# Second mixer's projections in a two-layer encoder: plain 32-bit matrix products replaced by three products over split operands

## The reference, cut to what matters

```python
def gla_mixer(h, w_in, w_gate2, b_gate2, gla_norm_g, w_out):     # h: (1, 512, 1024), the second mixer
    proj = h @ w_in                                              # (1024, 3088)
    q, k, v, g, z = jnp.split(proj, [512, 1024, 2048, 3072], axis=-1)
    log_a = jax.nn.log_sigmoid(z @ w_gate2 + b_gate2) / 16.0
    ...                      # chunks of 64 rows: state = state * decay + k_dec.T @ v;  o = q @ state
    o = o * lax.rsqrt(jnp.mean(o * o, axis=-1, keepdims=True) + EPS) * gla_norm_g
    o = o.reshape(B, S, 1024) * jax.nn.silu(g)
    return o @ w_out                                             # (1024, 1024)

# the trunk
x = x + even_mixer(rmsnorm(x, ln_mix[0]), ...)   # first mixer
x = x + peer(rmsnorm(x, ln_ffn[0]), ...)         # first expert stage
x = x + gla_mixer(rmsnorm(x, ln_mix[1]), ...)    # second mixer
x = x + peer(rmsnorm(x, ln_ffn[1]), ...)         # second expert stage
return rmsnorm(x, ln_final)
```

## Time and profile before

| | |
|---|---|
| Time, median of 3 runs | 2854.05 us (2853.29 to 2854.83) |
| Span of the profiled execution | 2852.1 us, 1.95 us under that median |
| PE busy | 2831.2 us (99%) |
| DVE busy | 2282.9 us (80%) |
| ACT busy | 1015.6 us (36%) |
| POOL busy | 750.5 us (26%) |

### The profile page before, as it was taken

The page is one execution under the profiler, slowest core; times in us unless marked ns, Lnnn a source line. Parts: engine busy times, 40 slices in busy tenths (PEclk is TensorE's granted clock), DMA queues, the critical chain, the costliest instruction groups (busy, mean ns, idle before and its releaser), DMA issues.

```text
span 2852.1 us, 39729 instructions
## 1 busy us (share of the span) xinstructions
PE 2831.2 (99%) x14626; PEld 1528.0 (54%) x14722; DVE 2282.9 (80%) x4310; ACT 1015.6 (36%) x1350; POOL 750.5 (26%) x518
## 2 busy tenths in 40 slices
PE   9999999999999999999999999999999999999999
PEld 5455555556666444444544465555566664444444
DVE  6955899997888999999611258999978888999996
ACT  2253232334555333333321232223345543333333
POOL 0000233421111554545000002333211115455450
PEclk9999999999999999999999999999999999999999
DMA  4213677867997999999321236777679979999993
GB/s 158 89 47 142 242 280 279 293 239 273 320 311 291 398 395 393 398 400 396 134 89 59 76 142 234 276 291 277 240 285 311 310 286 403 391 398 398 392 397 152
DMA packets 214835, 776.01 MB, mean 272 GB/s; under 512 B 15508, under 2 KB 101912, under 8 KB 194744
## 3 DMA queue, kind: packets, MB, share of 16 engines
q1 hardware_dynamic: 50096, 416.89, 38.2%
q0 software_dynamic: 73728, 268.47, 25.5%
q10 hardware_dynamic: 90888, 89.14, 9.0%
HBM read 681.90 MB, written 92.54 MB: 272 GB/s over the span
## 4 chain that ended last, share of the span: by engine, by line
PE 93%; issue 2%; PEld 1%; DVE 1%; DMA 1%; ACT 1%; DVEq 0%; POOL 0%; PEldq 0%; SPq 0%; ACTq 0%
PE ps L1819 29%; PE ps L1750 12%; PE ps L1749 12%; PE ps L1748 12%; PE ps L1722 8%; PE ps L1411 5%; PE ps L1402 4%; PE ps L1432 4%; PE ps L1801 2%; PE ps L1800 2%; PEld ps L1819 1%; PE ps L1758 1%; DMA arena<-in_ur,arena 1%; PE ps L1528 1%; PE ps L1465 0%
## 5 line engine op out<-in xcount | busy, mean ns | idle before, releaser
L1819 PE MATMUL ps<-arena 128*128 128x512 bf16 x4488 | 985.3, 379 | 6.7 <-DVE arena L1272 1.5
L500 POOL DMA_INDIRECT arena<-in_ur,arena x256 | 351.8, 1374 | 1582.8 <-DVE arena L1110 928.0
L1819 PEld LDWEIGHTS ps<-arena 128*128 128x128 bf16 x4584 | 448.2, 98 | 542.8 <-issue 3.5
L1083 DVE TENSOR_TENSOR arena<-arena 128x1024 bf16<-128x1024 f32 x512 | 611.3, 1220 | 116.6 <-ACT arena L723 93.7
L1750 PE MATMUL ps<-xnh,arena 128*128 128x384 bf16 x2048 | 667.6, 326 | 0.0
L1749 PE MATMUL ps<-xnl,arena 128*128 128x384 bf16 x2048 | 667.5, 326 | 0.0
L1748 PE MATMUL ps<-xnh,arena 128*128 128x384 bf16 x2048 | 667.4, 326 | 0.0
L723 ACT ACTIVATE arena<-arena 128x1024 bf16<-128x1024 f32 x512 | 524.2, 1048 | 120.0 <-PE ps L1819 98.8
L500 POOL DMA_INDIRECT arena<-in_v,arena x256 | 397.7, 1554 | 401.8 <-DVE x_res L1119 341.6
L1119 DVE SCALAR_TENSOR_TENSOR x_res<-arena,x_res 128x1024 f32<-128x1024 f32 x256 | 328.5, 1283 | 21.1 <-issue 0.9
L749 ACT ACTIVATE arena<-ps 128x384 f32<-128x384 f32 x256 | 125.8, 491 | 565.3 <-PE ps L1750 565.3
(11 more groups left out here) (219 smaller groups left out, 2294.0 us busy)
## 6 DMA issues: line engine op xcount, KB each, us to landing
arena<-in_v SPq DMA_DIRECT2D x64, 2048.0 KB, 10.3
arena<-in_u SPq DMA_DIRECT2D x62, 2048.0 KB, 10.2
h_scratch<-arena ACTq DMA_DIRECT2D x60, 768.0 KB
arena<-h_scratch SPq DMA_DIRECT2D x60, 768.0 KB, 8.6
arena<-gate_scratch SPq DMA_DIRECT2D x64, 640.0 KB, 6.8
arena<-in_wmix SPq DMA_DIRECT2D x14, 2048.0 KB, 8.0
gate_scratch<-xnT ACTq DMA_DIRECT2D x10, 2048.0 KB
gate_scratch<-arena ACTq DMA_DIRECT2D x10, 2048.0 KB
```

What stands on the lines that cost most here:

```text
L500: pool.indirect_dma_start(ring[n % NBUF], None, ur_d[L] if g < P else vr_d[L], at).then_inc(gat_in[n % NBUF], 16)
L1083: dve.tensor_tensor(lo[:, s], raw[s // TPG][:, s % TPG], hi[:, s], ALU.subtract).then_inc(lo_ready, 1)
L1819: last = pe.matmul(ps[:, 2 + 2 * tt + dh], c, v[:, TPG * s + q, dh * 512:(dh + 1) * 512], start=start and c is ch and v is hi, stop=stop a ...
```

## The change

The projections of `mixer1` (not z, not the small products, not the scan) are no longer one 32-bit product. Each operand is split into a high part, rounded to the type float32r, and the rest. The product is high x high, high x rest, and rest x high, all in float32r: 24 matmuls for a unit where there were 8 of 32 bits.

- ACT rounds each weight block in four pieces of 128 x 1024 (`weights_hi`), DVE subtracts in four pieces, in place over the block (`weights_lo`). Both stand at fixed places of the two engines' programs.
- The normalized tokens go to `x_hi`, written as float32r by the same instructions as before; DVE then makes the rest from PSUM (`norm_rest`), eight instructions a tile. The heads' outputs are treated in the same way (`heads_out`, four more instructions a tile on DVE, for both halves).
- The z unit stays 32-bit, with the tokens in two parts: 16 matmuls for 8.
- A unit waits for all four high pieces of its block before its first matmul, and for all four rest pieces before its last eight.
- The buffers in the arena are laid out anew. SP's first load of the second expert stage's query weights waits for the readouts (`go_done`), not for `kdec_ready`. It still stands behind the loads of blocks 9 to 15 in SP's program.

```diff
+        w_lo = [rounded(f"w_lo{s}", A_RAW + 4096 * s, KD, 512) for s in range(2)]
+        w_hi = [rounded(f"w_hi{s}", 30208 + 4096 * s, KD, 512) for s in range(2)]
...
-                    sp.wait_ge(kdec_ready, TT)
+                    sp.wait_ge(go_done, TT)
...
+            def weights_hi(b):                      # ACT
+                act.wait_ge(w_in[b % 2], 16 * (b // 2 + 1))
+                for p in range(PIECES):
+                    at = slice(2 * p, 2 * p + 2)
+                    act.activation(w_hi[b % 2][:, at], wblk[b % 2][:, at], ACT.Copy).then_inc(w_high, 1)
...
             def mixer1():                           # ACT
+                weights_hi(SPLIT0)
                 norm(2)
...
                 act.activation(g_ab, g_ab, ACT.Ln, bias=1.0).then_inc(lg_abs, 1)
+                weights_hi(SPLIT0 + 1)
                 unit_out(g_qT[:, 3], scale=float(P) ** -0.5)
...
                 unit_out(g_k[:, 1])
+                weights_hi(SPLIT0 + 2)
...
                         unit_out(g_v[:, tt, b * 512:(b + 1) * 512])
+                        if tt == 1:
+                            weights_hi(SPLIT0 + 3 + b)
...
                     unit_out(g_g[:, tt, b * 512:(b + 1) * 512], ACT.Silu)
+                    if tt == 1:
+                        weights_hi(SPLIT0 + 5 + b)
...
                     heads_out(tt)
+                weights_hi(SPLIT0 + 7)
...
+            def norm_rest(k, tt):                   # DVE
+                dve.wait_ge(xt_low, TT * k + tt + 1)
+                dve.drain()
+                for kd in range(KD):
+                    at = kd % (KD // 2) * P
+                    last = dve.scalar_tensor_tensor(x_low(kd)[:, tt * P:(tt + 1) * P],
+                                                    ps[:, turn_bank(k, tt) + kd // (KD // 2), at:at + P],
+                                                    cols[:, ...gain...],
+                                                    x_hi[:, kd, tt * P:(tt + 1) * P].bitcast(F32), ALU.mult, ALU.subtract)
+                last.then_inc(xt_rest, 1)
+            def weights_lo(b, pieces=range(PIECES)):
+                for p in pieces:
+                    at = slice(2 * p, 2 * p + 2)
+                    dve.wait_ge(w_high, PIECES * (b - SPLIT0) + p + 1)
+                    dve.tensor_tensor(w_lo[b % 2][:, at], wblk[b % 2][:, at], w_hi[b % 2][:, at].bitcast(F32),
+                                      ALU.subtract).then_inc(w_low, 1)
...
                     dve.tensor_tensor(xp, xp, ps[:, j % 2], ALU.add).then_inc(o_free, 1)
+                    if m == 1 and step < 2:
+                        weights_lo(SPLIT0 + 7, range(2 * step, 2 * step + 2))
...
                 if L == 0:
+                    weights_lo(SPLIT0)
                     norm_tile(2, 0)
...
                         norm_high(2, tt - 1)
                         norm_tile(2, tt)
+                        norm_rest(2, tt - 1)
...
                     norm_high(2, TT - 1)
+                    norm_rest(2, TT - 1)
...
+            def split_tokens(b, tt):                # PE; split_columns, q_half and project_split alike
+                weights_rounded(b)                  # all four pieces of w_high
+                bank = unit_bank()
+                at = slice(tt * P, (tt + 1) * P)
+                for kd in range(KD):
+                    pe.matmul(bank, x_hi[:, kd, at], w_hi[b % 2][:, kd], start=kd == 0, stop=False)
+                    pe.matmul(bank, x_low(kd)[:, at], w_hi[b % 2][:, kd], start=False, stop=False)
+                weights_rest(b)                     # all four pieces of w_low
+                for kd in range(KD):
+                    last = pe.matmul(bank, x_hi[:, kd, at], w_lo[b % 2][:, kd], start=False, stop=kd == KD - 1)
+                last.then_inc(p_done, 1)
...
+                weights_rounded(b)                  # ahead of the first q_half
+                weights_rest(b)
...
+                pe.wait_ge(xt_rest, 2)
                 q_banks = unit_bank(), unit_bank()
                 q_half(q_banks[0], 0, halves[0])
                 turned(2, TT - 1)
                 q_half(q_banks[1], 1, halves[0])
                 all_turned(2)
+                pe.wait_ge(xt_rest, TT)
                 for h in range(2):
                     q_half(q_banks[h], h, halves[1]).then_inc(p_done, 1)
```

More of the change, by code:

```diff
@@ L11 @@
 U32 = mybir.dt.uint32
+F32R = mybir.dt.float32r
 ALU = mybir.AluOpType
@@ L272, in build @@
         xn_split = sem("xn_split")
+        xt_rest = sem("xt_rest")
+        w_high = sem("w_high")
+        w_low = sem("w_low")
         p_done = sem("p_done")
@@ L530, in norm_low @@
                 for kd in range(KD // 2):
-                    last = act.activation(xnT[:, kd, tt * P:(tt + 1) * P], ps[:, turn_bank(k, tt), kd * P:(kd + 1) * P], ACT.Copy,
+                    dst = x_hi if k == 2 else xnT
+                    last = act.activation(dst[:, kd, tt * P:(tt + 1) * P], ps[:, turn_bank(k, tt), kd * P:(kd + 1) * P], ACT.Copy,
                                           scale=cols[:, C_GAIN + KD * k + kd:C_GAIN + KD * k + kd + 1])
@@ new lines, in split_tokens @@
+            def split_tokens(b, tt):
+                weights_rounded(b)
+                bank = unit_bank()
+                at = slice(tt * P, (tt + 1) * P)
+                for kd in range(KD):
+                    pe.matmul(bank, x_hi[:, kd, at], w_hi[b % 2][:, kd], start=kd == 0, stop=False)
+                    pe.matmul(bank, x_low(kd)[:, at], w_hi[b % 2][:, kd], start=False, stop=False)
+                weights_rest(b)
+                for kd in range(KD):
+                    last = pe.matmul(bank, x_hi[:, kd, at], w_lo[b % 2][:, kd], start=False, stop=kd == KD - 1)
+                last.then_inc(p_done, 1)
@@ new lines, in project_split @@
+            def project_split(b0, counts, between):
+                for step, (tt, dh) in enumerate(out_steps[1]):
+                    b = b0 + dh
+                    weights_rounded(b)
+                    j = outs[0]
+                    outs[0] += 1
+                    pe.wait_ge(o_free, j - 1)
+                    if dh == 0:
+                        pe.wait_ge(tr_free, counts[tt])
+                    at = slice(tt * P, (tt + 1) * P)
+                    for kd in range(KD):
+                        pe.matmul(ps[:, j % 2], x_hi[:, kd, at], w_hi[b % 2][:, kd], start=kd == 0, stop=False)
+                        pe.matmul(ps[:, j % 2], o_lo[:, kd, at], w_hi[b % 2][:, kd], start=False, stop=False)
+                    weights_rest(b)
+                    for kd in range(KD):
+                        last = pe.matmul(ps[:, j % 2], x_hi[:, kd, at], w_lo[b % 2][:, kd], start=False, stop=kd == KD - 1)
+                    last.then_inc(o_done, 1)
+                    if step and out_steps[1][step - 1][1] == 1:
+                        pt = out_steps[1][step - 1][0]
+                        if pt == 0:
+                            pe.wait_ge(tr_free, HEADS + 2 * TT)
+                        turned(3, pt)
+                    if step == after[1]:
+                        between()
@@ L1601, in q_half @@
                 def q_half(bank, h, at):
+                    cols_at = slice(h * P, (h + 1) * P)
                     for kd in range(KD):
-                        last = pe.matmul(bank[:, at], wblk[b % 2][:, kd, h * P:(h + 1) * P], xnT[:, kd, at],
-                                         start=kd == 0, stop=kd == KD - 1)
+                        pe.matmul(bank[:, at], w_hi[b % 2][:, kd, cols_at], x_hi[:, kd, at], start=kd == 0, stop=False)
+                        pe.matmul(bank[:, at], w_hi[b % 2][:, kd, cols_at], x_low(kd)[:, at], start=False, stop=False)
+                    for kd in range(KD):
+                        last = pe.matmul(bank[:, at], w_lo[b % 2][:, kd, cols_at], x_hi[:, kd, at],
+                                         start=False, stop=kd == KD - 1)
                     return last
                 halves = slice(0, T // 2), slice(T // 2, T)
+                weights_rounded(b)
+                weights_rest(b)
                 pe.wait_ge(xt_low, TT * 2 + 2)
                 pe.wait_ge(xt_high, TT * 2 + 2)
-                arrived(b)
+                pe.wait_ge(xt_rest, 2)
                 q_banks = unit_bank(), unit_bank()
@@ L1622, in mixer1 @@
                     at = slice(kd % 4 * ZR, (kd % 4 + 1) * ZR)
-                    last = pe.matmul(bank[at], wblk[Z_BLOCK % 2][:, kd, 0:ZR], xnT[:, kd], start=kd < 4, stop=kd >= 4)
+                    wz = wblk[Z_BLOCK % 2][:, kd, 0:ZR]
+                    pe.matmul(bank[at], wz, x_hi[:, kd].bitcast(F32), start=kd < 4, stop=False)
+                    last = pe.matmul(bank[at], wz, x_low(kd).bitcast(F32), start=False, stop=kd >= 4)
                 last.then_inc(p_done, 1)
                 z_unit = unit[0]
-                by_columns(b, 2)
+                split_columns(b, 2)
                 pe.wait_ge(p_free, z_unit)
@@ L1712, in other_heads @@
                     heads(3)
```

(3 more changed lines are left out.)

86 lines of the change are left out of this document (62 added, 24 removed).

## The result

| | before | after |
|---|---|---|
| Time, median | 2853.67 us (4 runs) | 2826.68 us (4 runs) |
| Ratio | | 0.9901, 95% interval 0.9886 to 0.9917 |
| Span of the profiled execution | 2852.1 us | 2823.2 us |
| From block 8's transfer (issue) to the second stage's first queries | 288.72 us | 259.54 us |

The kernel became 27.0 us faster, 1.0%. I forecast 38.1 us faster. One run of the four, 2919.59 us at a lower clock throughout, is out of the ratio; the median of the other three is 2826.42 us.

A forecast was written before the change was run, and what follows sets the result against it. PE was taken to bound the kernel, 93% of the span's chain. Savings of 52.4 us less waits of 14.3 gave -38.1, so 2816.0 us against 2854.05, with 8 in 10 for 2808 to 2828.

The forecast's parts named there:

- 30 units: Projections on PE: each unit takes 24 float32r matmuls, 5.18 us for 6.90, in all -51 us.
- (b): Mixer entry: block 8's rounding stands ahead of the norm on ACT, so PE's first transposes wait, +1.1 us.
- (c): Turn into the mixer: DVE's added token rests make PE wait before the last transposes and second token half, +2.8 us.
- (d): Block 9: its rounding stands behind the logarithm on ACT, so PE idles before key unit 0, +6.4 us.
- (e): After block 9's wait: the granted clock falls as in the first mixer, +1.5 us, range 0 to 3.
- (f): Output projection: PE waits for DVE's longer heads_out, the last turn and a bank, +2.5 us.
- I take one pass for float32r: PE pace: a 512-column float32r matmul takes one pass, 0.216 us like bfloat16, bounds 0.213 to 0.43.
- (a): Blocks 10 to 14: roundings and rests hidden; PE would wait for a bank if a rounding took over 4.5 us.
- (g): No cost from SP's later query-weight load, behind block 15's load anyway, nor from POOL, whose gathers start long after.
- The full hiding of waits: Rival: all waits are hidden, -52.4 us, 2801.7 us; chance 0.04.
- The load in the open: Rival: one pass, but each weight load of 0.108 us isn't hidden, 2897 us; chance 0.08 together with two passes.
- the two-pass case: Rival: unhidden load and two passes (0.43 us), units of 10.3 us, near 2965; chance 0.08 together with the one-pass load case.

The follow-up runs named there:

- e_dve9: The changed kernel with block 9 rounded by DVE, ahead of its subtraction, instead of by ACT behind the logarithm; 2819.04 us.
- e_probe: The changed kernel with ten short series of unused matmuls (float32r, bfloat16, 32-bit) added on PE behind the output projection; float32r at 512 columns took 0.2267 us each.
- e_twice: The changed kernel with ACT rounding every piece of blocks 10 to 13 twice; 2831.93 us.
- e_entry_q: The changed kernel with the first tile's norm ahead of block 8's split, and the last two q_half taking the rest-of-tokens passes last; 2826.14 us, stretch 257.3 us.
- e_tail: The changed kernel with DVE's heads_out(1) moved ahead of scale_heads(3) alone; 2827.73 us by one run, stretch 259.9 us.
- e_all: The changed kernel with the order changes of e_dve9, e_entry_q and e_tail together; 2815.91 us, 0.9863 of the kernel before.

## Why the prediction was right, and what it missed

The time, 2826.7, lies inside the range of 2808 to 2828, at its upper end; the sign and the mechanism were right, the size 11 us too good. By the prediction's own terms, each difference read between marks of the two chains and timelines:

| term | forecast | measured | from |
|---|---|---|---|
| 30 units | -51 | -43 | 6.87 to 5.44 us a unit |
| `q_half` | -3.3 | -2.3 | 96 at 0.120 us for 13.8 |
| z | +1.85 | +1.8 | 3.6 us for 1.85 |
| (b) entry | +1.1 | +0.8 | first transposes' matmuls 15.73 us after the transfer's issue, for 14.90 (1403.58); by their weight loads, which no longer lie under other work, 14.68 |
| (c) the turn | +2.8 | +2.0 | 0.29 + 1.68 |
| (d) block 9 | +6.4 | +5.95 | the bracket at 1460.23 |
| (e) the clock | +1.5 | +2.0 | e_dve9: 7.5 less 5.5, the brackets 5.95 and 0.46; also key unit 0 in 7.65 us for 5.44, 2.2 |
| (f) output projection | +2.5 | +1.8 | 1.20 + 0.56 |
| not assigned | | +1.75 | the difference to the stretch's -29.2 |

Of the last line about half is what the five brackets of (c), (d) and (f) leave out, 0.17 us each, 0.85.

- **The step that was mis-sized is the pace.** "I take one pass for float32r" was right: one record, one pass. Its size was off, 0.227 us for 0.216, outside the 0.213 to 0.222 that I gave the forecast's own range. 720 x 0.0107 = 7.7 us, and 1 us more in the `q_half`. I took the bfloat16 row for nearest, and had no row that would bound a fixed cost; e_probe shows it at 256, 384 and 512 columns.
- **Weight loads are hidden.** In e_probe matmuls of 128 columns, each with its own load, go at 0.110, so a load takes that or less, and at 512 columns load and pass together take 0.227, not the 0.32 of the rival. The Trainium skill's rule ("TensorE: Matmul & The Clock Gate", Part 3, The mechanism), that loads overlap only with another row group, does not hold here for 4-byte weights either.
- **(a) was right in what it forecast and wrong in its margin**, as e_twice showed: doubling ACT's rounding costs nothing in blocks 10 to 12. The place with a narrow margin is block 9, where the decay unit stands behind the rounding.
- **(b), (c), (d), (f) hold to 0.8 us each.** They came from reading the order of each engine's program against the rows, not from busy times: after the change DVE was busy for 108 of the 244 us from 1404 to 1648 and still made PE wait five times. e_entry_q, e_tail, e_dve9 and e_all took the larger ones away, one by one and then together, without taking away work. That (c) and (f) came out smaller since PE, with its slower pace, came later is my reading; no run tests it.
- **(e)** stood on one row of the first mixer; e_dve9 shows cause and size at the place itself. In the six other profiles with the wait unchanged (5.95 to 5.97 us) the window from 1460 to 1470 shows 0.66 to 0.77, and from key unit 0 to the second half of L1786 it is 10.7 to 11.1 us where this profile has 10.21. So the loss is 2 to 3 us, not a constant, and this profile's is the smallest of the seven. Nor does the length of a wait alone set it: behind the 1.68 us of (c) and the 1.20 of (f) the clock stays at 1.00 in this profile's windows (1420 to 1436, 1595 to 1650), while the row of the first mixer had 0.86 behind 1.48.
- **(g)** nothing, as forecast: the second stage took 1175.1 us (1648.11 to the end of the span) for 1174.7.
- **The other rivals.** The full hiding of waits, 2801.7, would with the measured pace be near 2811, or 245.2 us by the stretch; e_all is at 2816 and 248.4, and of these 3.2 us the waits that the change brought and that are left (0.29, 0.46 and 0.57) are 1.3, or 1.8 with what their brackets leave out. The load in the open and the two-pass case are out by the rows above.

What stays open: the origin of the fixed 0.011 us, and the 0.9 us that nothing assigns.

## What to carry to other kernels

When work moves off the bounding engine onto free ones, its price is its place in their programs: walk each engine's order, write down when each piece becomes ready and when the bound engine asks for it, and look first at the one place where the new piece stands behind a long chain (here a logarithm with two table loads). If such a piece can be done by another engine that is idle at that moment, most of the wait can go without any work saved (here 5.5 of 5.95 us). And take a new instruction form's pace as unknown by 5% even when the number of its passes is right: over 720 of them that was 8 us, more than any one wait.

## What the runs showed of the hardware that was not expected

- A float32r matmul costs 0.011 us more than a bfloat16 one of the same columns: 0.227 us at 512 columns, 0.120 at 256, for 0.216 and 0.109. The Trainium skill ("TensorE: Matmul & The Clock Gate", Back-to-back issue gap) gives columns / 2.4 GHz plus 2.5 ns for the isolated gap, which is 0.216 and 0.109, and about 0.131 for 512 columns in a sustained stream of loads and matmuls: the bfloat16 series, though such a stream, agree with the first and not with the second, the float32r series with neither, and the measurement decides.
- With 64 weight columns for 128 the matmul became no faster (0.230 for 0.227 us).
- An idle stretch of 5.95 us on PE cost 2 to 3 us more in lowered clock (0.66 to 0.79 in the 10 us from 1460), one of 2.86 us some 1.7 us. In e_all, where no wait is over 0.6 us, the clock stayed at 1.00 in every window of the stretch, and so it did in e_dve9, with waits of 1.68 and 1.20 us at its entry and end.
- DVE and ACT write 4-byte float32r results at the price of 2-byte ones: subtraction 1219 ns for 1220, copy on ACT 1048 for 1048 ns, 1024 elements a partition.
